# Softmax division moved from a scaled identity to GpSimd, and memory rows scaled ahead of their transposes

## The chip, the cores and the metric

One core of one Trainium2 chip runs the whole program in one launch. The metric is the device time of the program in microseconds (us). Five engines run their own instruction streams and meet at semaphores: TensorE (PE; its weight loads are listed as PEld), VectorE (DVE), ScalarE (ACT), GpSimd (POOL) and SyncE (SP, which here only starts transfers).

## The reference, cut to what matters

Two layers (`DEPTH = 2`) over 256 tokens of width 1024, everything in float32. Each layer is: a gated feed-forward block, a mixing block of three branches, a cross attention to 256 memory rows, and a second feed-forward block. The parts that the change touches are the two softmaxes of the mixing block and the normalisation of the memory rows:

```
# fox branch, 8 heads of width 64, blocks of 128 queries
logits = q k^T * 64**-0.5 + bias;  p = softmax(logits);  o = p @ v
# dsa branch, 8 heads over a shared latent c of width 128
logits = q_lat c_sel^T * 64**-0.5 + t5 bias;  p = softmax(logits);  o_lat = p @ c_sel;  o = o_lat @ w_uv
# memory cross attention
mem_h = rms_norm(mem, mem_norm[l]);  k, v = split(mem_h @ w_mkv)
```

## The kernel before, in words

Every weight is read once from HBM, 1 MB (a "unit") at a time into a ring of three slots. ScalarE copies a unit to its rounded part `w_hi` (L491), VectorE subtracts to get the rest `w_lo` (L499), and TensorE multiplies three times per tile (hi by hi, lo by hi, hi by lo; L1500, L1522, L1537 and L1575/L1577). The order of the work on each engine is written out by hand and is the same for all units.

In the mixing block a stream of 16 attention steps (`STREAM = 16`, positions `s` = 0 to 15, plus 3 to drain) is woven between weight units. A step is two heads of one block of 128 queries. Steps 0 to 7 are the fox branch, 8 to 15 the dsa branch; within each, the first four see 128 keys per head and the last four 256. At position `s` TensorE does in this order: `pt` of step s-1 (transposes the probabilities), `pv` of s-2 (times the values), `uv` of s-3 (dsa only), `qk` of s (the logits), `ql` of s+1 (dsa only), for s = 13 to 16 `mt` (normalises and transposes a quarter of the memory rows), and then one weight unit of 48 matmuls, the "filler" `FILL[s]`.

The softmax of a step: VectorE takes the logits from PSUM into `lg` and their minimum (L1336 or L1345, L1349), ScalarE takes the exponential in place with its row sum (L1013), VectorE the reciprocal `ri` (L1361). GpSimd then builds a 128 by 128 identity scaled by `ri` for each of the two heads (`over_sum`, L750), and TensorE multiplies the unscaled `lg` with it, as an ordinary float32 matmul (L1696), which divides and transposes at once. ScalarE copies the result to `pt` (L789). After L750 GpSimd adds the causal mask to a bias (L705, steps 1 to 3) or makes the next `t5_score` (L717, from step 7 on). VectorE in the same position splits a weight unit in two parts (L499), the second right behind the reciprocal, and picks the top keys (L1375, L1377) or merges branches (L1192, L1196, L1199).

The memory rows `mem_x`: ScalarE takes squares at s = 10 (L1026); GpSimd makes `rstd` and with it a scaled identity `diag` (`power`, L697); TensorE at s = 13 to 16 multiplies the rows with `diag` (`rows_over_rms`, L1455).

PSUM results of these jobs turn through 4 banks in the order of the jobs: a job may start when the job four before it has been taken out of its bank (`wait_free`, `wait_jobs`). The names to follow in the code are `over_sum`, `over_sum_ready`, `power`, `rows_over_rms` and `wait_free`. Further on, in the cross attention, the kernel has already a `pe.transpose` of probabilities that VectorE has divided in place (L1773).

Of the kernel before, what the change touches and what calls it, by code (L numbers as in the profile page):

```python
# [23 lines left out]
ACT = mybir.ActivationFunctionType  # L24
# [3 lines left out]
P = 128  # L28
# [207 lines left out]
def block_kernel(nc, t, out):  # L236

    ctx = ExitStack()
    with ctx:
# [3 lines left out]
        def at(name, shape, dtype=F32, over=None, skip=0):  # L243

            nbytes = 4 * int(np.prod(shape[1:]))
            if over is None:
                start = at.top
                at.top += (nbytes + 31) // 32 * 32
            else:
                start = place[over] + skip  # L250
            place[name] = start
            return nc.alloc_sbuf_tensor_at(name, shape, dtype, offset=start)
# [33 lines left out]
        mem_q = at("mem_q", [P, BT, SEQ], over="kc")  # L286
        junk = at("junk", [P, 2 * TT, 512], over="qc")
        qi = at("qi", [P, BT, SEQ])
        over_sum = at("over_sum", [P, 2, 2, P], over="qi")
        t5_score = at("t5_score", [P, 2, 2, SEQ], over="qc")  # L290
        vc = at("vc", [P, TT, BW])
        ki = at("ki", [P, SEQ])
# [62 lines left out]
        def sem(name):  # L355
            return ctx.enter_context(nc.semaphore(name))
# [52 lines left out]
        lg_ready = sem("lg_ready")  # L409
        exp_ready = sem("exp_ready")  # L410
        ri_ready = sem("ri_ready")
        over_sum_ready = sem("over_sum_ready")
        causal_ready = sem("causal_ready")
        score_ready = sem("score_ready")
        t5_score_ready = sem("t5_score_ready")
# [249 lines left out]
        def _(g):  # L665
# [17 lines left out]
            def power(l, n, tt, diagonal=True):  # L683

                step = (SUMS_OF + SUMS_OF[:1])[n] // TT
                g.wait_ge(ssq_ready, l * SSQ + (sum(SUMS_OF[:n]) + step * (tt + 1)))
                if step == 2:
                    g.tensor_tensor(ms[:, tt:tt + 1], ssq[:, tt, 0:1], ssq[:, tt, 1:2], ALU.add)  # L688
                else:
                    g.tensor_tensor(ms[:, tt:tt + 1], ssq[:, tt, 0:1], one_lat[:], ALU.mult)  # L690
                g.drain()
                g.tensor_scalar(ms[:, tt:tt + 1], ms[:, tt:tt + 1], EPS, None, ALU.add)
                g.drain()
                e = g.tensor_tensor(rstd[:, tt:tt + 1], ms[:, tt:tt + 1], minus_half[:], ALU.pow)
                if diagonal:
                    g.drain()  # L696
                    e = g.tensor_scalar(diag[:, tt, :], ident[:], rstd[:, tt:tt + 1], None, ALU.mult)  # L697
                    if n in (0, 5, 6):
                        e = g.tensor_scalar(half_rstd[:, tt:tt + 1], rstd[:, tt:tt + 1], 0.5, None, ALU.mult)
                e.then_inc(rstd_ready, 1)  # L700
# [40 lines left out]
            for l in range(DEPTH):  # L741
                for n in (1, 2):
                    for tt in range(TT):
                        power(l, n, tt, n != 2)
                for s in range(STREAM):
                    if s == 0:
                        g.wait_ge(bias_landed, l * 32 + 32)
                        causal_bias(0)
                    g.wait_ge(ri_ready, l * STREAM + s + 1)
                    g.tensor_tensor(over_sum[:, s % 2, :, :], ident[:].unsqueeze(1).to_broadcast([P, 2, P]),  # L750
                                    ri[:, s % 2, :].unsqueeze(2).to_broadcast([P, 2, P]), ALU.mult)\
                     .then_inc(over_sum_ready, 1)
                    if 0 < s < 4:
                        causal_bias(s)
                    if 8 <= s + 1 < STREAM:
                        bias_and_score(l, s + 1)
                    if s == 10:
                        for tt in range(TT):
                            power(l, 3, tt)
                for n in range(4, len(SUMS_OF) + 1):  # L760
                    for tt in range(TT):
                        power(l, n, tt)
# [3 lines left out]
        def _(a):  # L766
# [128 lines left out]
            for l in range(DEPTH):  # L895
# [87 lines left out]
                for s in range(STREAM + 3):  # L983
                    if 0 <= s - 1 < STREAM:
                        k = s - 1
                        n_s = (k % 8) // 4 + 1
                        copy_out(l, ("pt", k), pt[:, k % 2, :, 0:n_s, :],
                                 ps(("pt", k))[:, 0:2 * n_s * P].rearrange("p (h c t) -> p h c t", h=2, t=P))
                    if 0 <= s - 2 < STREAM:
                        k = s - 2  # L990
                        blk, h, base, m = slot_of(k)
                        if k < 8:
                            wait_done(a, l, ("pv", k))
                            a.activation(o_hi[1][base:base + HD, m:m + 2, blk * P:blk * P + P],
                                         ps(("pv", k))[base:base + HD, 0:2 * P].rearrange("p (h t) -> p h t", h=2),
                                         ACT.Copy).then_inc(o_part, 1)
                        else:
                            copy_out(l, ("pv", k), ol[:, k % 2, :, :],
                                     ps(("pv", k))[:, 0:2 * P].rearrange("p (h t) -> p h t", h=2))
                    if 8 <= s - 3 < STREAM:  # L1000
                        k = s - 3
                        blk, h, base, m = slot_of(k)
                        wait_done(a, l, ("uv", k))
                        a.activation(o_hi[0][base:base + HD, m:m + 2, blk * P:blk * P + P],
                                     ps(("uv", k))[base:base + HD, 0:2 * P].rearrange("p (h t) -> p h t", h=2),
                                     ACT.Copy).then_inc(o_part, 1)
                    if s >= 1:
                        splits(a, split_hi, l, FILL[s - 1])
                    if s < STREAM:
                        s_len = P * ((s % 8) // 4 + 1)  # L1010
                        a.wait_ge(lg_ready, l * STREAM + s + 1)
                        for j in range(2):
                            e = a.activation(lg[:, s % 2, j, 0:s_len], lg[:, s % 2, j, 0:s_len], ACT.Exp, scale=-1.0,  # L1013
                                             bias=nm[:, s % 2, j:j + 1], accum_out=sm[:, s % 2, j:j + 1])
                        e.then_inc(exp_ready, 1)
                    if 8 <= s + 1 < STREAM:
                        k = s + 1
                        copy_out(l, ("ql", k), ql[:, k % 2, :, :],
                                 ps(("ql", k))[:, 0:2 * P].rearrange("p (h t) -> p h t", h=2))
                    if s == 8:  # L1020

                        a.dma_start(mem_x[:], t["mem"][0].rearrange("(a p) d -> p a d", p=P)).then_inc(mem_landed, 16)
                    if s == 10:
                        a.wait_ge(mem_landed, l * 16 + 16)
                        for b in range(2 * TT):
                            a.activation(mem_junk[:, b, :], mem_x[:, b // 2, (b % 2) * 512:(b % 2) * 512 + 512], ACT.Square,  # L1026
                                         scale=D ** -0.5, accum_out=ssq[:, b // 2, b % 2:b % 2 + 1]).then_inc(ssq_ready, 1)
                    if 13 <= s < 17:
                        for k in (2 * (s - 13), 2 * (s - 13) + 1):
                            norm_hi(l, 4, k, mem_hi, ("mt", k // 2))  # L1030
                    filler(l, FILL[s])
# [415 lines left out]
        def _(pe):  # L1447
# [188 lines left out]
            for l in range(DEPTH):  # L1636
# [50 lines left out]
                for s in range(STREAM + 3):  # L1687
                    if 0 <= s - 1 < STREAM:
                        k = s - 1
                        n_s = (k % 8) // 4 + 1  # L1690
                        pe.wait_ge(over_sum_ready, l * STREAM + k + 1)
                        wait_free(pe, l, ("pt", k))
                        for j in range(2):
                            for c in range(n_s):
                                col = (j * n_s + c) * P
                                mm = pe.matmul(ps(("pt", k))[:, col:col + P], lg[:, k % 2, j, c * P:c * P + P],  # L1696
                                               over_sum[:, k % 2, j, :], start=True, stop=True)
                        mm.then_inc(job_done, 1)
                    if 0 <= s - 2 < STREAM:
                        k = s - 2  # L1700
# [38 lines left out]
                                           qb[base:base + HD, m + j, blk * P:blk * P + P], start=True, stop=True)  # L1739
                        mm.then_inc(job_done, 1)  # L1740
                    if 13 <= s < 17:
                        pe.wait_ge(rstd_ready, l * 12 + 8)
                        wait_free(pe, l, ("mt", s - 13))
                        for k in (2 * (s - 13), 2 * (s - 13) + 1):
                            for tt in range(TT):
                                mm = rows_over_rms(l, ("mt", s - 13), k, tt, mem_x)
                        mm.then_inc(job_done, 1)
                    filler(l, FILL[s])
                for name in AFTER:
# [61 lines left out]
```

## Time and profile before

| what | value |
|---|---|
| median of 3 runs | 1472.14 us (1470.92 to 1473.11) |
| the profiled execution's own time | 1473.94 us |
| its span in the trace | 1472.0 us |
| PE busy | 1432.3 us, 97% |
| DVE / ACT / POOL busy | 64% / 53% / 9% |
| granted TensorE clock | 0.993 of full speed |
| mean HBM rate | 165 GB/s |

The span is what the trace covers; the time has some 2 us more around it. A busy share is an average over stages, and a matmul's record overlaps the next one's: what a matmul takes of the engine is the distance from one start to the next, not the duration in the record. Times in rows of the timeline are from the span's start; a row with "x4" holds four instructions one after the other, and its second column is from the first start to the last end. Rows in which idle time precedes name it in brackets with what ended it.

### The profile page before, as it was taken

The numbers are of one execution on the slowest core, as the hardware profiler recorded it, in microseconds if no ns is written. First come the engines' busy times: TensorE is split into PE (matmuls) and PEld (weight loads), VectorE is DVE, ScalarE is ACT, GpSimd is POOL, SyncE is SP. The second block draws the span as 40 slices with busy tenths as digits, with TensorE's granted clock in tenths as the row PEclk, the third lists the DMA queues.
The fourth block names the chain that finished last, engine by engine and source line by source line (L and its number), as shares of the span: only waits on it lengthen the run. The fifth ranks groups of instructions, "written<-read, shape, count | busy, mean of one in ns | idle before, by whom it ended". The sixth has DMA issues, their size and how long they took to land.

```text
span 1472.0 us, 24395 instructions
## 1 busy us (share of the span) xinstructions
PE 1432.3 (97%) x9101; PEld 1282.8 (87%) x9101; DVE 935.2 (64%) x1451; ACT 786.3 (53%) x1394; POOL 127.0 (9%) x223
## 2 busy tenths in 40 slices
PE   6999989999999999999999999999999999999997
PEld 5888879989999898888888888898998999888886
DVE  5666665866546557666676666667755465666665
ACT  5545555655544456545565545565555445655553
POOL 2010000021310100000000000000233001000001
PEclk9999999999999999999999999999999999999999
DMA  8677654644335535666566667454353454466661
GB/s 230 186 203 215 193 146 140 200 144 144 115 115 172 172 116 171 189 182 199 172 185 187 184 187 220 142 165 152 115 166 94 132 182 144 139 185 191 183 188 72
DMA packets 286066, 243.41 MB, mean 165 GB/s; under 512 B 14280, under 2 KB 263544, under 8 KB 285984
## 3 DMA queue, kind: packets, MB, share of 16 engines
q1 hardware_dynamic: 283856, 236.77, 53.1%
q10 hardware_dynamic: 1600, 4.25, 0.9%
q0 software_dynamic: 528, 1.26, 0.5%
q8 instruction: 56, 0.92, 0.2%
q14 instruction: 26, 0.21, 0.0%
HBM read 241.18 MB, written 1.27 MB: 165 GB/s over the span
## 4 chain that ended last, share of the span: by engine, by line
issue 62%; PE 29%; DVE 4%; POOL 1%; POOLq 1%; DMA 1%; DVEq 1%; ACT 1%; ACTq 0%
PE work L1500 16%; PE work L1575 2%; PE work L1522 2%; PE work L1696 1%; PE work L1577 1%; PE acc L1537 1%; PE work L1730 1%; PE work L1706 1%; PE work L1727 1%; DVE w_lo L499 1%; POOLq L696 1%; PE acc L1455 1%; POOL diag L697 1%; DVE score L1302 1%; PE work L1644 0%
## 5 line engine op out<-in xcount | busy, mean ns | idle before, releaser
L499 DVE TENSOR_TENSOR w_lo<-raw,w_hi 128x1024 fp32r<-128x1024 f32 x444 | 532.8, 1221 | 103.4 <-ACT w_hi L491 102.2
L1575 PE MATMUL work<-act,w_hi 128*128 128x512 f32 x1408 | 499.0, 398 | 8.3 <-DVE w_lo L499 4.3
L491 ACT ACTIVATE w_hi<-raw 128x1024 fp32r<-128x1024 f32 x444 | 452.2, 1051 | 26.0 <-PE acc L1537 25.6
L1577 PE MATMUL work<-act,w_lo 128*128 128x256 f32 x1408 | 396.0, 281 | 0.0
L1575 PEld LDWEIGHTS work<-act,w_hi 128*128 128x128 f32 x1408 | 265.5, 189 | 72.1 <-issue 9.3
L1500 PE MATMUL work<-act,w_hi 128*128 128x256 f32 x1696 | 316.6, 285 | 4.2 <-DVE act L1097 3.3
L1500 PEld LDWEIGHTS work<-act,w_hi 128*128 128x128 f32 x1696 | 267.4, 191 | 11.4 <-issue 7.5
L1577 PEld LDWEIGHTS work<-act,w_lo 128*128 128x128 f32 x1408 | 267.4, 190 | 1.6
L1500 PE MATMUL work<-act,w_lo 128*128 128x256 f32 x848 | 239.8, 283 | 0.0
L796 ACT ACTIVATE gu_s<-work 128x256 f32<-128x256 f32 x176 | 58.0, 381 | 209.4 <-PE work L1577 209.4
L1500 PEld LDWEIGHTS work<-act,w_lo 128*128 128x128 f32 x848 | 162.5, 192 | 0.0
L1119 DVE TENSOR_TENSOR gu_s<-gu_s,work 128x256 f32<-128x256 f32 x176 | 66.2, 417 | 138.6 <-ACT gu_s L796 138.6
L1537 PE MATMUL acc<-w_hi,h_hi 128*128 128x512 f32 x320 | 125.4, 392 | 0.0
L1537 PE MATMUL acc<-w_lo,h_hi 128*128 128x512 f32 x320 | 125.3, 392 | 0.0
L1537 PE MATMUL acc<-w_hi,h_lo 128*128 128x512 f32 x320 | 125.2, 391 | 0.0
L806 ACT ACTIVATE h_hi<-h_f 128x256 fp32r<-128x256 f32 x80 | 33.4, 418 | 102.6 <-PE acc L1537 86.9
L688 POOL TENSOR_TENSOR ms<-ssq 128x1 f32<-128x1 f32 x22 | 4.9, 225 | 892.6 <-ACT junk L771 892.6
L1537 PEld LDWEIGHTS acc<-w_hi,h_lo 128*128 128x128 f32 x320 | 60.1, 188 | 13.3
L1537 PEld LDWEIGHTS acc<-w_hi,h_hi 128*128 128x128 f32 x320 | 60.1, 188 | 13.3
L1537 PEld LDWEIGHTS acc<-w_lo,h_hi 128*128 128x128 f32 x320 | 60.1, 188 | 11.4
L1138 DVE TENSOR_TENSOR h_lo<-h_f,h_hi 128x256 fp32r<-128x256 f32 x80 | 33.7, 421 | 49.5 <-ACT h_hi L806 49.5
L750 POOL TENSOR_TENSOR over_sum<-ident,ri 128x256 f32<-128x256 f32 x32 | 42.1, 1315 | 251.5 <-DVE ri L1361 251.5
(230 smaller groups left out, 1837.5 us busy)
## 6 DMA issues: line engine op xcount, KB each, us to landing
raw<-in_ffn_w_gu SPq DMA_DIRECT2D x176, 512.0 KB, 5.0
raw<-in_w_in SPq DMA_DIRECT2D x52, 1024.0 KB, 5.2
raw<-in_ffn_w_down SPq DMA_DIRECT2D x44, 1024.0 KB, 5.0
raw<-in_w_branch SPq DMA_DIRECT2D x12, 1024.0 KB, 5.0
raw<-in_w_mkv SPq DMA_DIRECT2D x8, 1024.0 KB, 5.3
raw<-in_w_out SPq DMA_DIRECT2D x8, 1024.0 KB, 4.8
raw<-in_w_mq SPq DMA_DIRECT2D x4, 1024.0 KB, 5.5
raw<-in_w_mo SPq DMA_DIRECT2D x4, 1024.0 KB, 4.9
```

The lines of the kernel that those rows point to most:

```text
L491: eng.activation(halves(w_hi, slot, kind, part), halves(raw, slot, kind, part), ACT.Copy)\
L499: eng.tensor_tensor(halves(w_lo, slot, kind, part), halves(raw, slot, kind, part), halves(w_hi, slot, kind, part).bitcast(F32), ALU.subtra ...
L750: g.tensor_tensor(over_sum[:, s % 2, :, :], ident[:].unsqueeze(1).to_broadcast([P, 2, P]), ri[:, s % 2, :].unsqueeze(2).to_broadcast([P, 2 ...
L796: a.activation(gu_s[:, c, g, :], work[:, 2 * c + g, SEQ:2 * SEQ], ACT.Copy).then_inc(cross_ready, 1)
L806: a.activation(dst[:, c, :], h_f[:, c, :], ACT.Copy).then_inc(h_hi_ready, 1)
L1119: v.tensor_tensor(gu_s[:, c, g, :], gu_s[:, c, g, :], work[:, 2 * c + g, 0:SEQ], ALU.add)\
L1138: v.tensor_tensor(lo[:, c, :], h_f[:, c, :], hi[:, c, :].bitcast(F32), ALU.subtract)\
L1500: mm = pe.matmul(out_ps, ww[:, slot, first:first + width], xx[:, k, :], start=(k == 0 and n == 0), stop=(k == kn - 1 and n == 2))
L1522: mm = pe.matmul(out_ps(tt), xx[:, k, tt * P:tt * P + P], ww[:, slot, k * 256 + cols[0]:k * 256 + cols[1]], start=(k == 0 and n == 0), sto ...
L1537: mm = pe.matmul(acc[:, tt, nh * 512:nh * 512 + 512], xx[:, k0 + kk, tt * P:tt * P + P], ww[:, slot, kk * D + nh * 512:kk * D + nh * 512 + ...
L1575: pe.matmul(work[:, 2 * c + g, :], w_hi[:, slot, at_w:at_w + P], act[:, :, k, :], start=(k == 0), stop=False, skip_group_check=True)
L1577: mm = pe.matmul(work[:, 2 * c + g, 0:SEQ], w_lo[:, slot, at_w:at_w + P], act_hi[:, k, :], start=False, stop=(k == KT - 1), skip_group_che ...
```

## The change

GpSimd no longer builds `over_sum`; it multiplies `lg` in place by the reciprocal, over as many keys as the step has (2 x 128 or 2 x 256 elements per partition). TensorE then transposes `lg` with the plain identity. For the memory rows, `power` leaves out the scaled identity; at s = 11 ScalarE multiplies each of the two row tiles by its `rstd` in place, and TensorE at s = 13 to 16 transposes the scaled rows with the plain identity.

```diff
-                    g.tensor_tensor(over_sum[:, s % 2, :, :], ident[:].unsqueeze(1).to_broadcast([P, 2, P]),
-                                    ri[:, s % 2, :].unsqueeze(2).to_broadcast([P, 2, P]), ALU.mult)\
-                     .then_inc(over_sum_ready, 1)
+                    s_len = P * ((s % 8) // 4 + 1)
+                    g.tensor_tensor(lg[:, s % 2, :, 0:s_len], lg[:, s % 2, :, 0:s_len],
+                                    ri[:, s % 2, :].unsqueeze(2).to_broadcast([P, 2, s_len]), ALU.mult)\
+                     .then_inc(p_ready, 1)
...
-                            power(l, 3, tt)
+                            power(l, 3, tt, False)
...
+                    if s == 11:
+                        a.wait_ge(rstd_ready, l * 12 + 8)
+                        for tt in range(TT):
+                            a.activation(mem_x[:, tt, :], mem_x[:, tt, :], ACT.Copy, scale=rstd[:, tt:tt + 1])\
+                             .then_inc(mem_scaled, 1)
...
-                        pe.wait_ge(over_sum_ready, l * STREAM + k + 1)
+                        pe.wait_ge(p_ready, l * STREAM + k + 1)
                         wait_free(pe, l, ("pt", k))
...
-                                mm = pe.matmul(ps(("pt", k))[:, col:col + P], lg[:, k % 2, j, c * P:c * P + P],
-                                               over_sum[:, k % 2, j, :], start=True, stop=True)
+                                mm = pe.transpose(ps(("pt", k))[:, col:col + P], lg[:, k % 2, j, c * P:c * P + P], ident[:])
...
-                        pe.wait_ge(rstd_ready, l * 12 + 8)
+                        pe.wait_ge(mem_scaled, (l + 1) * TT)
                         wait_free(pe, l, ("mt", s - 13))
...
-                                mm = rows_over_rms(l, ("mt", s - 13), k, tt, mem_x)
+                                mm = pe.transpose(ps2(("mt", s - 13))[:, k % 2, tt * P:tt * P + P],
+                                                  mem_x[:, tt, k * P:(k + 1) * P], ident[:])
```

## Rows read from the trace of the kernel before

**Rows 1.** The page's first part: busy us, share of the span, instructions.
```profile
PE 1432.3 (97%) x9101; PEld 1282.8 (87%) x9101; DVE 935.2 (64%) x1451; ACT 786.3 (53%) x1394; POOL 127.0 (9%) x223
```

**Rows 2.** Windows: attention of layer 0; span, busy PE, PEld, DVE, ACT, POOL, PEclk, DMA, GB/s.
```profile
289.00:447.00 158.00, 155.86 (x1218) 145.83 (x1217) 95.55 (x176) 83.75 (x179) 37.02 (x35) 1.00 0.40 129
```

**Rows 3.** Source views of L1696, L1455 and L1773: count, duration ns min/median/max.
```profile
L1696 PE MATMUL work<-over_sum,lg x192: 270/275/377, 297.0 to 1153.7; 128*128 128x128 f32 x192
L1455 PE MATMUL work<-diag,mem_x x64: 273/275/377, 401.0 to 1156.3; 128*128 128x128 f32 x64
L1773 PE MATMUL work<-ident,lg x32: 270/272/273, 529.7 to 1260.5; 128*128 128x128 f32 x32
```

**Rows 4.** Timeline of PE: groups of L1696 and of transposes, each with what follows.
```profile
312.10 0.60 PE L1696 MATMUL work<-over_sum,lg 128*128 128x128 f32 x4
312.63 0.65 PE L1706 MATMUL work<-pt,vc 128*64 128x128 f32 x4
...
397.33 1.05 PE L1696 MATMUL work<-over_sum,lg 128*128 128x128 f32 x8
398.22 0.61 PE L1710 MATMUL work<-pt,c_nat 128*128 128x128 f32 x4
...
529.74 1.03 PE L1773 MATMUL work<-ident,lg 128*128 128x128 f32 x8
530.53 0.36 PE L1522 MATMUL work<-w_hi,mem_hi 128*128 128x256 f32 x1
```

**Rows 5.** Timeline of PE at s = 2: `pv` of step 0.
```profile
305.03 0.65 PE L1706 MATMUL work<-pt,vc 128*64 128x128 f32 x4 [0.24 <-ACT vc L789]
```

**Rows 6.** Timeline of PE at s = 14, and PE's row of the waits.
```profile
412.35 1.16 PE L1455 MATMUL work<-diag,mem_x 128*128 128x128 f32 x8
413.81 0.39 PE L1500 MATMUL work<-act,w_hi 128*128 128x256 f32 x1 [0.29 <-DVE o_lo L1355]
...
PE work L1500 <- DVE o_lo L1355: 0.9, 4, 0.3
```

**Rows 7.** Timeline of POOL at s = 2 and 3 (L750).
```profile
309.15 1.84 POOL L750 TENSOR_TENSOR over_sum<-ident,ri 128x256 f32<-128x256 f32 x1 [5.78 <-DVE ri L1361]
...
316.78 0.61 POOL L750 TENSOR_TENSOR over_sum<-ident,ri 128x256 f32<-128x256 f32 x1 [5.09 <-DVE ri L1361]
```

**Rows 8.** Timeline at s = 6: L750, the split beside it, and `pt` behind.
```profile
342.25 1.84 POOL L750 TENSOR_TENSOR over_sum<-ident,ri 128x256 f32<-128x256 f32 x1 [8.30 <-DVE ri L1361]
342.41 1.21 DVE L499 TENSOR_TENSOR w_lo<-raw,w_hi 128x1024 fp32r<-128x1024 f32 x1
...
345.04 1.05 PE L1696 MATMUL work<-over_sum,lg 128*128 128x128 f32 x8
```

**Rows 9.** Timeline at s = 12 (layer 0): POOL, DVE, and `qk` of step 13.
```profile
394.21 1.21 DVE L499 TENSOR_TENSOR w_lo<-raw,w_hi 128x1024 fp32r<-128x1024 f32 x1
...
395.85 1.28 POOL L717 TENSOR_TENSOR t_score<-t,score 128x512 f32<-128x512 f32 x1
396.21 1.47 DVE L1199 TENSOR_TENSOR merged<-merged,gate 128x512 f32<-128x512 f32 x1
...
397.61 0.68 DVE L1196 SCALAR_TENSOR_TENSOR gate<-gate,work 128x512 f32<-128x512 f32 x1
...
398.36 0.69 DVE L1199 TENSOR_TENSOR merged<-merged,gate 128x512 f32<-128x512 f32 x1
...
399.34 1.13 PE L1730 MATMUL work<-c_t,ql 128*128 128x256 f32 x4
```

**Rows 10.** Timeline of ACT at s = 11 and 12, and `w_hi`'s row of the groups.
```profile
384.22 0.36 ACT L789 ACTIVATE ql<-work 128x256 f32<-128x256 f32 x1
...
388.56 0.60 ACT L870 ACTIVATE gate<-work 128x512 f32<-128x512 f32 x1 [3.98 <-PE work L1500]
...
L491 ACT ACTIVATE w_hi<-raw 128x1024 fp32r<-128x1024 f32 x440 | 448.8, 1053 | 26.0 <-PE acc L1537 25.6
```

**Rows 11.** Timeline of POOL: the last `power` of the memory rows.
```profile
381.78 0.62 POOL L697 TENSOR_SCALAR diag<-ident,rstd 128x128 f32<-128x128 f32 x1 [0.17 <-issue]
```

More of the change, by code:

```diff
@@ L288, in block_kernel @@
         qi = at("qi", [P, BT, SEQ])
-        over_sum = at("over_sum", [P, 2, 2, P], over="qi")
         t5_score = at("t5_score", [P, 2, 2, SEQ], over="qc")
@@ L411, in block_kernel @@
         ri_ready = sem("ri_ready")
-        over_sum_ready = sem("over_sum_ready")
+        p_ready = sem("p_ready")
+        mem_scaled = sem("mem_scaled")
         causal_ready = sem("causal_ready")
```

## The prediction

> **What bounds the kernel now.** I read the page's busy shares first: TensorE works 97% of the span, no other engine above 64% [rows 1]. Then the window of the stretch that holds the attention steps of layer 0 (layer 1 repeats it), since a mean over the whole span may hide a stage with another limit: there TensorE is busy 155.9 of 158.0 us, VectorE 96 and ScalarE 84 [rows 2]. So TensorE sets the pace in the changed stretch too, and what the change takes from TensorE's stream shortens the kernel unless an engine that hands it work becomes late. The weights arrive at 129 GB/s there [rows 2], under the 165 of the whole span, so loads have room. Third, the source views and the timeline of the changed instructions give their price, and the brackets on PE's rows show where it waits.
>
> **TensorE, the terms.** The program issues 96 division matmuls (per layer 8 steps of 2 and 8 steps of 4), but the trace has 192 records for L1696; 32 for the memory rows, but 64 records for L1455. The `pe.transpose` of L1773, with the same kind of operand (`lg` against the plain identity), is issued 32 times and has 32 records [rows 3]. So one float32 matmul runs as two passes and a transpose as one. The mean duration, 275 and 272 ns, tells nothing of the difference; distances do. Eight passes of L1696 last 1.05 us up to the last end, so (1.05 - 0.275)/7 = 0.111 us from start to start; eight transposes last 1.03, so (1.03 - 0.272)/7 = 0.108 us; and the next group starts 0.89 us after the first of eight passes, 0.79 after the first of eight transposes [rows 4]. One pass of 0.11 us is saved for each matmul: 0.22 us in a step of two (four passes, now 0.53 us to the next group), 0.44 us in a step of four. If all of it reached the end: 128 x 0.11 = 14.1 us.
>
> The Trainium skill, "TensorE: Matmul & The Clock Gate", Part 4 (PE-mode transpose), gives about 275 ns for a transpose in a kernel and says that access latency dominates it. The records here agree in length (272 ns), but the starts are 108 ns apart, so that latency overlaps in a row of transposes. By the page's figure as a price the change would lose; that is one of the rivals below.
>
> **What of it is lost in waits on PSUM banks.** A shorter group helps only if the next job may start.
> - `pt` of step 1: `pv` of step 0 waited 0.24 us for ScalarE's copy of `vc`, which starts when the filler ahead of `pt` ends [rows 5]. `pt` shortens, the wait grows by as much: 0 of 0.22.
> - `mt` at s = 13 and 14: the filler behind it needs the bank that VectorE empties at L1355, behind the logits of `qk`. At s = 14 it waited 0.29 us, and the waits' row has four such waits, 0.9 us in all: s = 13 and 14 of both layers [rows 6]. That moment hangs on `qk`, which is ahead of `mt`, so `mt`'s 0.44 us turns into waiting: 0. At s = 15 and 16 there is no such wait, 2 x 0.44.
> - `pt` of step 12: `qk` of step 13 needs the bank of the second half of `bc0`, which VectorE empties at L1199. That ends at 398.36 + 0.69 = 399.05, and `qk` starts at 399.34 [rows 9]. With 0.44 us less in front of it `qk` reaches its place at 398.90 and waits. It is lost here, and possibly more (below).
> - The other steps have no bracket and reach a bank that is free for longer.
>
> Per layer: narrow steps 0, 2, 3, 8, 9, 10, 11, 7 x 0.22 = 1.54; wide steps 4 to 7, 13, 14, 15, 7 x 0.44 = 3.08; `mt` 0.88; together 5.5. Two layers: 11.0 us.
>
> **GpSimd, the division.** For narrow steps it multiplies 256 elements as before (1.52 us or so). For wide steps it is 512 instead of 256, which no row of L750 shows. From below, nothing: it might cost the same. The nearest row is L717 on 512 elements, 1.28 us [rows 9]; from above, twice the longest L750, 3.68 us [rows 7]. The records of L750 are of two kinds, 0.61 and 1.84 us for one shape [rows 7]. At s = 6 it begins at 342.25, VectorE's split L499 runs from 342.41 to 343.62, and L750 ends at 344.09, that is 0.47 us after L499 [rows 8]; at s = 12 the pattern is turned round, L1199 starts at 396.21 beside a running L717 and lasts 1.47 instead of 0.69 us, to 0.55 us after the end of L717 at 397.13 [rows 9]. So the two engines exclude each other in these operations, and the net length is some 0.6 us for 256 and 1.28 us for 512. I take 1.28, since it is a two-input operation of this size on this engine with a broadcast operand.
>
> The Trainium skill, "SBUF — State Buffer", section "SBUF: two separate sides", calls the pair of ports that VectorE and GpSimd share an exclusive lock, held for the whole instruction by whoever starts first. The rows agree, and the rule speaks against this change: the wide division holds VectorE off for longer.
>
> Its deadline is `pt`. At s = 6 the split ends at 343.62, so the division ends at 344.90, and `pt` starts at 345.04 [rows 8]: 0.14 us to spare. At s = 12 it ends at 395.42 + 1.28 = 396.70 against 397.33 [rows 4, 9]. Steps 4 and 15 resemble these; in the other wide steps GpSimd comes first or `pt` is later. So nothing on the path, narrowly; if the cover were gone each further 0.1 us costs 0.1 us a step.
>
> Behind the division are queued, on GpSimd, `t5_score` of the next step (L717), needed only at the next `qk`, and on VectorE, by the exclusion, the second split and what follows. That is free except at s = 12: L1199 now starts when the division ends (396.70) or, if L717 takes its turn first, at 397.98. In the first order it ends at 397.4, L1196 of the second half at 398.3, and the second L1199 waits for L717 (397.4 to 398.7) and ends at 399.4: `qk` of step 13 is 0.06 us later than before. In the second the ends are 398.7, 399.4 and 400.1: 0.75 us later. I take 0.3 us for each layer, 0.6 in all; the bounds are 0.1 and 1.5.
>
> **ScalarE, the memory rows.** Two copies with a scale over 128x1024 elements; the nearest row has 1.053 us for that size, so 2.1 us a layer. They stand behind the copy of `ql` at 384.22 + 0.36 = 384.58, and the next instruction, the gate at 388.56, sat idle 3.98 us in wait of TensorE [rows 10]. 384.58 + 2.1 = 386.7: hidden, with 1.9 us over. The new wait for `rstd` ends at once: GpSimd had ended even the `diag` that now goes at 382.40 [rows 11]. `mt` needs the rows at s = 13, about 401. Without cover it would be 4.2 us for both layers on ScalarE, and it is the bound of this term; I take 0. `diag` off GpSimd (0.62 us each) gives nothing: TensorE used it 20 us later. No DMA is added or moved.
>
> **Sum.** -11.0 + 0.6 = -10.4 us. The profiled execution took 1473.94 us (span 1472.0 plus 1.9 around), so 1463.5; the median of the runs shown is 1.8 us lower, 1472.14, which gives **1461.7 us**. Changes under 0.2% (2.9 us) count as none.
>
> **The rivals.**
> 1. *The division is twice as long*, 2.56 us net. For it: the rows of GpSimd are rough, and in-place operands are not L717's. Against: 0.47 us of L750 behind the split. Room behind the end of the split: 345.04 - 343.62 = 1.42 us at s = 6 and 397.33 - 395.42 = 1.91 at s = 12 [rows 4, 8, 9]; two wide steps of each kind wait: 2 x 1.14 + 2 x 0.65 = 3.6 us a layer, 7.2 in all. -11.0 + 7.2 = -3.8: **1468.3**. Chance 0.09.
> 2. *The division ends above the time before.* The same place with twice the longest record, 3.68 us: 2 x 2.26 + 2 x 1.77 = 8.1 a layer, 16.1 in all, +5.1: **1477.2**. It decides from 4T - 6.66 = 5.5, T = 3.04 us. Against: L717's 1.28. Chance 0.02.
> 3. *Transposes do not overlap* and cost their 272 ns each: a group of four 1.09 instead of 0.89, of two 0.54 instead of 0.53, 16 + 8 groups of four: 24 x 0.2 = +4.8 us: **1477**. Against: the eight of L1773 in 1.03 us. Chance 0.02.
> 4. *Nothing changes on TensorE*, the transpose being run as two passes: **1472 to 1473**. Against: 32 records for 32. Chance 0.03.
> 5. *Waits I count as lost are not*: VectorE's chain moves forward too, and all 14.1 us arrive: **1458.0**. Against: the brackets. Chance 0.08.
>
> **Chances and range.** Forecast 0.76, own range 1459.5 to 1464.5 (the bounds at s = 12 and 1 us for the medians). Faster: 0.76 + 0.09 + 0.08 = 0.93; same 0.03; slower 0.04. For 8 in 10 I widen to rival 5 and towards rival 1: 1458.5 to 1466.5.
>
> **What the profile after would show.** L1696 and the `mt` transposes with 96 and 32 records, eight passes now four, `pt` to `pv` about 0.31 us narrow and 0.45 to 0.54 wide; PE busy some 13 us less. The wide division 1.3 us where GpSimd comes first and 2.0 to 2.5 where the split does, no PE wait on it beyond the first step's. The wait on `o_lo` L1355 grows from 0.9 us to about 2.5; `qk` of step 13 gets a wait. ScalarE's copies end before 388. The prediction is wrong if `pt` waits for the division in many steps, or if transposes are more than 0.15 us apart.

## The result, and the profile after

| | before | after |
|---|---|---|
| median, first comparison (6 runs each) | 1471.53 us | 1463.06 us |
| median, second comparison (18 and 5 runs) | 1471.47 us | 1461.31 us |
| ratio after/before, 95% interval | | 0.9943 [0.9931, 0.9956]; again 0.9921 [0.9907, 0.9934] |
| profiled execution: time, span | 1473.94, 1472.0 us | 1461.06, 1459.3 us |
| PE busy | 1432.3 us | 1415.9 us |

By the ratios the change gains 8.4 us in the first comparison (interval 6.5 to 10.2) and 11.6 in the second (9.7 to 13.7); the medians themselves are 8.5 and 10.2 us apart. 10.4 was forecast (1461.7 us).

The comparison that holds from run to run is a stretch of the trace: from the first `qk` of a layer to the first matmul of `mk0`, 16 steps and 18 fillers further. It is 157.98 us in layer 0 of before (288.94 to 446.92 in its timeline) and 152.12 after. The timeline of PE of the changed kernel, the two ends:

```profile
287.94 0.71 PE L1732 MATMUL work<-kc,qc 64*128 64x128 f32 x4
...
440.06 0.39 PE L1506 MATMUL work<-mem_hi,w_hi 128*128 128x256 f32 x1
```

That is 5.86 us. In layer 1 it was 159.69 us before and is 152.10 after. Of the 1.71 us by which layer 1 of before is longer than its layer 0, 1.50 are one filler in which the granted clock fell (last section) and 0.2 stand in front of `qk` of step 13 (told at s = 12, below). So layer 0 is taken as the measure: 5.86 us a layer, 11.7 in all. The stage behind it, to the transposes of the second feed-forward block (552.01 us in before), is 105.09 us in both profiles; the stages outside the stretch differ by up to 1 us either way (layer 0's first feed-forward 190.48 and 189.84, layer 1's second 187.31 and 188.23), as they do between two profiles of one kernel. So, within that scatter, the trace has the gain in the changed stretch alone.

The source views of the transposes after, against [rows 3] (L1702 was L1696, L1751 stands for L1455's matmuls of `mem_x`):

```profile
L1702 PE MATMUL work<-ident,lg x96: 270/272/328, 296.1 to 1140.6; 128*128 128x128 f32 x96
...
L1751 PE MATMUL work<-ident,mem_x x32: 272/273/330, 396.5 to 1142.6; 128*128 128x128 f32 x32
```

128 records have gone, and the durations are as before: it is the count that fell, not the length. The weight loads fell by the same 128 (PEld x9101 to x8973), so what goes is a pass together with its load; no run separates the two. The timeline of PE, a narrow `pt` group and a wide one, against [rows 4]:

```profile
310.85 0.38 PE L1702 MATMUL work<-ident,lg 128*128 128x128 f32 x2
311.16 0.65 PE L1711 MATMUL work<-pt,vc 128*64 128x128 f32 x4
...
393.01 0.60 PE L1702 MATMUL work<-ident,lg 128*128 128x128 f32 x4
393.45 0.61 PE L1715 MATMUL work<-pt,c_nat 128*128 128x128 f32 x4
```

0.31 us to the next group in place of 0.53, 0.44 in place of 0.89. What did not arrive stands in PE's waits after. Of the third row [rows 6] had 0.9 us; the first row belongs to other stages:

```profile
PE work L1506 <- DVE act L1103: 4.0, 4, 1.3
PE work L1702 <- POOL lg L751: 2.9, 2, 1.5
PE work L1506 <- DVE o_lo L1361: 2.9, 4, 0.8
PE work L1711 <- ACT vc L790: 0.9, 2, 0.5
...
PE work L1735 <- DVE merged L1205: 0.3, 2, 0.2
```

The wait on GpSimd, 2.9 us in 2 times, is that of the first step of each layer, as before. No other step waits for the division.

Laid over each other from the first `qk`, the fillers of layer 0 start earlier by these amounts (us, worked out from the starts in the two timelines; step 1 is the `pt` in position 2, and so on):

| part | forecast | measured |
|---|---|---|
| `pt` of step 0 | 0.22 | 0.26 |
| `pt` of step 1 (waits for `vc`) | 0 | 0.00 |
| `pt` of steps 2, 3 | 0.44 | 0.45 |
| `pt` of steps 4 to 7 | 1.76 | 1.69 |
| `pt` of steps 8 to 11 | 0.88 | 0.92 |
| `pt` of step 12 and `mt` at s = 13 | 0, less 0.3 | 0.24 |
| `pt` of step 13 and `mt` at s = 14 | 0.44 | 0.44 |
| `pt` of steps 14, 15, `mt` at s = 15, 16 | 1.76 | 1.85 |
| sum | 5.2 | 5.86 (rounded parts 5.85) |

### The profile page after: what moved, and what is told of

Read it like the earlier page. It is cut to its first block, busy times and chain, and to the rows that moved or that the text cites. A ratio compares the mean times of both kernels' runs of the same rounds, so it can differ in the third digit from the quotient of the medians.

```text
span 1459.3 us, 24135 instructions
## 1 busy us (share of the span) xinstructions
PE 1415.9 (97%) x8973; PEld 1265.0 (87%) x8973; DVE 935.3 (64%) x1451; ACT 789.1 (54%) x1398; POOL 131.6 (9%) x219
## 4 chain that ended last, share of the span: by engine, by line
issue 62%; PE 29%; DVE 4%; POOL 1%; POOLq 1%; DMA 1%; ACT 1%; DVEq 1%; ACTq 0%
PE work L1506 17%; PE work L1581 2%; PE work L1528 2%; PE work L1583 1%; PE acc L1543 1%; PE work L1735 1%; PE work L1711 1%; PE work L1732 1%; POOLq L696 1%; PE work L1702 1%; DVE w_lo L499 1%; POOL diag L697 1%; DVE score L1308 1%; PE acc L1461 1%; PE work L1650 0%
## 5 line engine op out<-in xcount | busy, mean ns | idle before, releaser
L751 POOL TENSOR_TENSOR lg<-lg,ri 128x256 f32<-128x256 f32 (+1 forms) x32 | 48.9, 1528 | 239.6 <-DVE ri L1367 239.6
L1543 PEld LDWEIGHTS acc<-w_lo,h_hi 128*128 128x128 f32 x320 | 60.1, 188 | 11.7
```

The lines of the kernel that those rows point to most:

```text
L751: g.tensor_tensor(lg[:, s % 2, :, 0:s_len], lg[:, s % 2, :, 0:s_len], ri[:, s % 2, :].unsqueeze(2).to_broadcast([P, 2, s_len]), ALU.mult)\
L1543: mm = pe.matmul(acc[:, tt, nh * 512:nh * 512 + 512], xx[:, k0 + kk, tt * P:tt * P + P], ww[:, slot, kk * D + nh * 512:kk * D + nh * 512 + ...
```

## The experiments

All stretches are from the first `qk` to `mk0`. Where the text speaks of the clock's fall, the granted clock had fallen in one filler of that layer, which makes the stretch 1.5 us longer; that is told in the last section, and the other layer is compared. Each ratio is to runs of before taken beside that kernel, so kernels of different experiments are compared by their stretches or ratios, not by their medians.

**1. The changed kernel again.**

> The changed kernel once more, in more rounds. In the two profiles the attention stretch (first qk to the first matmul of mk0) went from 157.98 and 159.69 us to 152.12 and 152.10, 1.7 us of it in layer 1 being a filler that was slow once in the profile of before. Theory (one TensorE pass of 0.11 us less per matmul, less the waits): 2 x 5.86 = 11.7 us less in the medians too, ratio 0.992. Rival (something of it is given back in other stages, as the medians of 1471.53 and 1463.06 would have it): 8.4 us less again, ratio 0.9943, and another stage longer by 3 us in its profile.

Measured: 1461.31 us, ratio 0.9921 [0.9907, 0.9934], which is 11.6 us less (the medians are 10.2 apart); stretches 152.12 and 153.62 us, the stages behind them 105.09 again. This interval holds the 11.7 us of the trace and not the rival's 8.4. Nothing is given back elsewhere in the profile: layer 1's 153.62 is the fall of the clock. Why the first six runs had 8.4, with an interval that doesn't hold 11.7, isn't shown: their mean granted clocks were 0.991 to 0.993, those of these five 0.992 to 0.996.

**2. The probabilities alone.** As after, but

```diff
-                            power(l, 3, tt, False)
+                            power(l, 3, tt)
...
-                                mm = pe.transpose(ps2(("mt", s - 13))[:, k % 2, tt * P:tt * P + P],
-                                                  mem_x[:, tt, k * P:(k + 1) * P], ident[:])
+                                mm = rows_over_rms(l, ("mt", s - 13), k, tt, mem_x)
```

and without ScalarE's copies.

> Only the probabilities: division on GpSimd and transposes in L1702; the memory rows as before, with diag. Theory (passes saved less waits): the memory part is worth 2 x 0.44 us a layer at s = 15 and 16 only, so this kernel keeps 5.0 of 5.9 us a layer: 10.0 us under before, the stretch 153.0 us. Rival (the memory transposes save all their passes, 1.76 us a layer): 8.2 us under before, the stretch 153.9 us.

Measured: 1462.05 us, ratio 0.9933 [0.992, 0.9947]; stretches 153.09 and 153.10 us, wait on `o_lo` 0.9 us. 4.89 us a layer from the probabilities, where the theory had 5.0.

**3. The memory rows alone.** As before, with the edits of `power`, ScalarE's copies and the `mt` transposes.

> Only the memory rows: scaled by ScalarE, transposed with the identity; over_sum as before. Theory: at s = 13 and 14 the filler waits for o_lo L1355 in place of the passes saved, at s = 15 and 16 two times 0.44 us arrive: 1.8 us under before, wait on o_lo 2.7 us in place of 0.9. Rival: all 16 passes a layer arrive, 3.5 us under before. Rival 2: the copies of 2.2 us on ScalarE are in the way: no gain or slower.

Measured: 1469.15 us, ratio 0.9984 [0.9974, 0.9995]; stretches 156.85 and 157.03 us, wait on `o_lo` 2.9 us. 1.13 and 0.95 us arrive. The `mt` groups themselves bring 0.44 us at s = 15, 0.50 at s = 16 and nothing at s = 13 and 14, that is 0.94 of the 1.76 us of passes in a layer; the rest is lost in the wait. What the stretches show beside it is not of this edit: the filler at s = 15 is 0.2 us shorter in both layers, and layer 1 loses 0.2 us in front of `qk` of step 13, as it does in before.

**4. Both edits, but ordinary matmuls with the identity.**

```diff
-                                mm = pe.transpose(ps(("pt", k))[:, col:col + P], lg[:, k % 2, j, c * P:c * P + P], ident[:])
+                                mm = pe.matmul(ps(("pt", k))[:, col:col + P], lg[:, k % 2, j, c * P:c * P + P], ident[:],
+                                               start=True, stop=True)
```

> The changed kernel with ordinary float32 matmuls against the identity in place of both transposes (two passes again); GpSimd still divides, ScalarE still scales. Theory: the whole gain is TensorE's passes, so this takes the time of before within 1 us (stretch 158.0 us) with the waits on o_lo back at 0.9 us. Rival: the division in place of over_sum costs or gains by itself: over 2 us away from before, with waits of TensorE on the division.

Measured: 1471.48 us, ratio 0.9993 [0.9982, 1.0004]; stretches 158.01 and 158.00 us, and the wait on `o_lo` is back at 0.9 us. The source view of L1702 has 192 records again:

```profile
L1702 PE MATMUL work<-ident,lg x192: 270/275/377, 295.6 to 1149.6; 128*128 128x128 f32 x192
```

The move of the division and of the scaling costs and gains nothing by itself; the whole gain is the pass that TensorE leaves out in its transpose mode.

**5. Every transpose of the probabilities twice.**

```diff
-                                mm = pe.transpose(ps(("pt", k))[:, col:col + P], lg[:, k % 2, j, c * P:c * P + P], ident[:])
+                                mm = [pe.transpose(ps(("pt", k))[:, col:col + P], lg[:, k % 2, j, c * P:c * P + P], ident[:]) for _ in range(2)][-1]
```

> The changed kernel with every transpose of the probabilities issued twice into the same place (96 more). Theory (a transpose in a row costs its 0.108 us, start to start): 48 x 0.108 = 5.2 us more a layer, of which the waits on vc (0.47) and on merged (0.17) take back 0.4: stretch 152.1 + 4.8 = 156.9 us, time 9.6 us over the changed kernel. Rival (a transpose costs its 0.272 us): 13 us a layer, 26 in all.

Measured: 1468.47 us, ratio 0.9973 [0.9963, 0.9984]; stretches 156.77 and 156.80 us, 4.7 more a layer. 48 transposes cost 4.7 us net of the waits that they fill, some 0.1 us each: the start-to-start distance is the price, the 272 ns of the record are not. By the ratios this kernel is 7.6 us over the changed one, where 9.6 was expected and the stretches have 9.3; with 0.001 of uncertainty in each ratio (1.5 to 2 us) that doesn't contradict them.

**6. One more multiplication ahead of the wide divisions.**

```diff
+                    if s_len == 2 * P:
+                        g.tensor_tensor(lg[:, s % 2, :, 0:s_len], lg[:, s % 2, :, 0:s_len],
+                                        ones[:, 0:2].unsqueeze(2).to_broadcast([P, 2, s_len]), ALU.mult)
+                        g.drain()
```

> The changed kernel with one more GpSimd multiplication (by ones) ahead of the division in the wide steps, that is 1.04 us more there with the drain. Theory (the division is hidden with the room of the trace, 0.5 us at s = 6, 0.6 at s = 4, 1.0 at s = 12, 0.9 at s = 15, over 1.7 elsewhere): TensorE waits 0.6 + 0.5 + 0.1 + 0.2 us a layer, and VectorE's merging at s = 12 is held up so that qk of step 13 waits up to 1 us more: 3 to 6 us over the changed kernel. Rival 1 (it was never near the path): within 1 us. Rival 2 (all eight wide steps pay in full): 16 x 1.04 = 17 us.

Measured: 1465.74 us, ratio 0.9958 [0.9946, 0.9971]; in layer 1, where the clock held, 155.36 us, 3.24 more than after. Layer 0 has 156.51 with the clock's fall of 1.48, so 2.9 more; the layers differ before `pt` of step 12, where TensorE waited 0.37 and 0.72 us for the division. TensorE's wait on POOL is 6.5 us in 10 times in place of 2.9 in 2. Step 6 in its timeline:

```profile
1059.81 2.27 POOL L752 TENSOR_TENSOR lg<-lg,ones 128x512 f32<-128x512 f32 x1 [5.70 <-DVE ri L1371]
...
1062.22 1.04 POOL L755 TENSOR_TENSOR lg<-lg,ri 128x512 f32<-128x512 f32 x1
...
1063.31 0.66 PE L1706 MATMUL work<-ident,lg 128*128 128x128 f32 x4 [0.56 <-POOL lg L755]
```

The division is hidden with about the room that the trace shows; four of the eight wide steps of a layer run out of it.

**7. VectorE empties `uv`'s bank ahead of the logits.** In VectorE's loop the block with L1361 (`o_lo` of step s-3) moves in front of the block that waits for `qk` of s; nothing else changes.

> The changed kernel with VectorE's L1361 (it empties the bank of uv) ahead of the logits of the position in place of behind them; VectorE idles there for TensorE's qk. Theory (the memory passes at s = 13 and 14 were lost in TensorE's wait on that bank): the waits of 0.66 and 0.80 us go, 1.4 us a layer, stretch 150.7 us, 2.8 us under the changed kernel. Rival: TensorE then waits for something else there (mt's or ol's bank), gain under 1 us.

Measured: 1455.25 us, ratio 0.9885 [0.9866, 0.9904]; stretches 150.15 and 150.12 us; once more, in five runs:

> The kernel olo_first once more, for an interval of its own: stretch 150.15 us (151.6 in a layer in which the granted clock falls behind the first division), 2 x 1.97 = 3.9 us under the changed kernel, ratio 0.9895 to before. Rival: the ratio of 0.9885 of four runs was luck and it is at 0.991 or above.

Measured: 1455.73 us, ratio 0.9897 [0.9881, 0.9914]; stretches 151.64 (with the clock's fall) and 150.16. The timeline at s = 13, of the changed kernel and then of this one:

```profile
396.48 0.66 PE L1751 MATMUL work<-ident,mem_x 128*128 128x128 f32 x4
...
397.80 0.39 PE L1506 MATMUL work<-act,w_hi 128*128 128x256 f32 x1 [0.66 <-DVE o_lo L1361]
```

```profile
393.13 0.42 DVE L1337 TENSOR_TENSOR o_lo<-work,o_hi 64x256 fp32r<-64x256 f32 x1 [0.41 <-ACT o_hi L1005]
...
394.00 0.69 DVE L1358 SCALAR_TENSOR_TENSOR lg<-work,t_score 128x512 f32<-128x512 f32 x1 [0.45 <-PE work L1735]
...
394.53 0.65 PE L1751 MATMUL work<-ident,mem_x 128*128 128x128 f32 x4
...
394.94 0.36 PE L1506 MATMUL work<-act,w_hi 128*128 128x256 f32 x1
```

L1337 runs in time that VectorE spent waiting for `qk`. From `mt` to the filler it was 1.32 us and is 0.41: 0.91 gained where the bracket said 0.66; at s = 14 it is 1.06 where the bracket said 0.80. A bracket counts from the modelled end of the last matmul. The group's record ends 0.66 us after its start, but without the wait the filler starts 0.41 us after it, so the bracket leaves out 0.25 us, and a loss of this kind is read from starts. That makes 1.97 us a layer, more than the 1.4 expected.

**8. In addition, `t5_score` ahead of the division.**

```diff
+                    if 8 <= s + 1 < STREAM:
+                        g.wait_ge(lg_ready, l * STREAM + s + 1)
+                        bias_and_score(l, s + 1)
                     g.wait_ge(ri_ready, l * STREAM + s + 1)
...
-                    if 8 <= s + 1 < STREAM:
-                        bias_and_score(l, s + 1)
```

> As the kernel before in this call, and GpSimd makes the next t5_score ahead of the division, once the logits of the position are out, in place of behind it. Theory: at s = 12 VectorE's L1205 is no longer held up by L717, TensorE's wait of 0.17 us before qk of step 13 goes, 0.2 to 0.3 us a layer: stretch 150.4 us, 0.5 us under the kernel before it. Rival: L717 now stands beside the first split of VectorE and in front of the division, so the division is late: a TensorE wait on it in some steps and no gain.

Measured: 1456.49 us, ratio 0.9892 [0.9873, 0.9912]; layer 1's stretch 150.14 us, layer 0's 151.62 with the clock's fall. Nothing gained, and the wait before `qk` of step 13 stays at 0.17: my theory of it fell. The rival fell too, for TensorE's wait on the division is still that of the first steps, 2.9 us in 2 times.

**9. The bank handed back one instruction earlier.** On top of 7, L1202, the only reader of the PSUM bank, frees it in place of L1205, and a new semaphore says when `gate` is free, the buffer in which ScalarE hands VectorE its factor for the merge. (`ba`, `bc` and `bb` are the three branches, `ba0` and `bc0` the first of their weight units.) The first version also had a drain, in which VectorE waits for its own writes, behind each half of `ba`.

> The kernel with L1361 ahead of the logits, and in the merging VectorE hands the PSUM bank back after the one instruction that reads it (L1202) in place of the next (L1205); a semaphore of its own says when the gate buffer is free. The kernel olo_first had TensorE waiting 0.18 us before qk of step 13, the end of VectorE's L1202 and L1205, which ran without a hold by GpSimd. Theory (that wait is VectorE's own chain of 2 x 0.7 us behind TensorE's last matmul of bc0, and the bank is what it hands on): the wait goes, and with it 0.2 to 0.3 us a layer, stretch 149.9 us in place of 150.15. Rival (the wait was for something else that comes at the same time): stretch unchanged.

Measured: 1456.22 us, ratio 0.9904 [0.9889, 0.9919]; stretches 150.24 and 150.22. The wait went and `qk` of step 13 gained 0.24 us, but `ql` of step 8 came 0.3 us later, behind the drain. Without it (ScalarE's waits for the new semaphore are left out here):

```diff
                         v.scalar_tensor_tensor(out=g2, in0=g2, scalar=1.0, in1=ps2((name, half)), op0=ALU.add,
-                                               op1=ALU.mult)
+                                               op1=ALU.mult).then_inc(bank_of((name, half)), 1)
                         v.drain()
-                        e = v.tensor_tensor(m2, m2, g2, ALU.add)
-                        e.then_inc(bank_of((name, half)), 1)
+                        v.tensor_tensor(m2, m2, g2, ALU.add).then_inc(gate_used, 1)
```

> As release_early, but without the drain that it put between the two halves of ba0 and ba1 (the gate's semaphore now counts the halves of bc and bb alone). In release_early the wait before qk of step 13 went and gave 0.24 us, and the drain held the second L1197 back by 0.21 us, so that ql of step 8 came 0.28 us later. Theory: without the drain the 0.24 us stays, stretch 149.9 us in both layers where the clock does not fall. Rival: 150.15 us as in olo_first.

Measured: 1454.94 us, ratio 0.9883 [0.9866, 0.9899]; stretches 149.91 and 149.92 us, as expected. The timeline in front of `qk` of step 13, layer 1: `qk` (L1737) now starts before L1208, which was L1205, has ended:

```profile
1107.15 0.69 DVE L1208 TENSOR_TENSOR merged<-merged,gate 128x512 f32<-128x512 f32 x1
...
1107.72 1.13 PE L1737 MATMUL work<-c_t,ql 128*128 128x256 f32 x4
```

This is the best version: 8.1 us a layer under before in the stretch, 16 us in the medians. From 7 its medians can't be told apart; the stretches can.

**10. ScalarE's copies doubled.** Each scaled copy preceded by a copy by 1 and a drain.

> The changed kernel with each of ScalarE's scaled copies of the memory rows preceded by a copy of the same rows by 1, 4.4 us in place of 2.2 us a layer at s = 11. Theory (the copies lie in ScalarE's idle time before the gate, 1.89 us of it left): the gate starts 0.3 to 0.5 us late, TensorE has room for that, stretch 152.1 us as before. Rival (ScalarE's copies are on the path): stretch 154.3 us.

Measured: one run, 1466.5 us; stretches 153.61 and 153.56, both with the clock's fall. That fall is over before the filler of s = 2: laid over the changed kernel from there to the end, every filler has the same distance within 0.05 us. ScalarE goes from its last copy to `gate` without idle time, and TensorE doesn't notice. The term is nothing even with twice the work.

## Why the prediction was right, point by point

**One pass for two.** Right, and shown by 4 and 5: the passes are the whole gain, 0.22 us in narrow and 0.44 to 0.45 in wide steps. PE's busy time fell by 16.4 us where some 13 was forecast.

**Lost in waits on banks.** `pt` of step 1 and `mt` at s = 13 and 14 gave 0, as forecast, and experiment 7 gave the latter back. One such wait I had missed: `ql` of step 8 needs `ba0`'s bank and lost 0.11 us of step 6's 0.44. (It was in experiment 9 that `ql` moved with VectorE's work on `ba0`.)

**The division.** The mechanism was right, the size too large: 1.04 us net, not 1.28. Timeline at s = 5 and 6, against [rows 8]:

```profile
331.19 1.04 POOL L751 TENSOR_TENSOR lg<-lg,ri 128x512 f32<-128x512 f32 x1 [5.75 <-DVE ri L1367]
331.60 1.71 DVE L499 TENSOR_TENSOR w_lo<-raw,w_hi 128x1024 fp32r<-128x1024 f32 x1
...
339.65 2.27 POOL L751 TENSOR_TENSOR lg<-lg,ri 128x512 f32<-128x512 f32 x1 [7.42 <-DVE ri L1367]
339.81 1.21 DVE L499 TENSOR_TENSOR w_lo<-raw,w_hi 128x1024 fp32r<-128x1024 f32 x1
...
342.43 0.60 PE L1702 MATMUL work<-ident,lg 128*128 128x128 f32 x4
```

Whoever is first holds the other off: at s = 5 the split takes 1.71 us in place of 1.21, at s = 6 the division 2.27 in place of 1.04. It ends 0.51 us before `pt`, where 0.14 was forecast.

**The failed term: s = 12.** The sum had "I take 0.3 us for each layer" lost beyond `pt`'s 0.44. Measured: 0.24 gained. The first error needed no experiment. By [rows 9] VectorE ended at 399.05, and the rows after show that `qk` starts 0.15 us behind that end (394.66, 394.81), so before it could have started at 399.20 in place of 399.34: of the 0.44 us, 0.14 were free even with VectorE as it was. The rest is that VectorE's second half begins 0.20 in place of 0.28 us after `pt`. The timeline of the changed kernel, against [rows 9]:

```profile
391.90 0.69 DVE L1205 TENSOR_TENSOR merged<-merged,gate 128x512 f32<-128x512 f32 x1
391.97 1.77 POOL L717 TENSOR_TENSOR t_score<-t,score 128x512 f32<-128x512 f32 x1
...
393.21 0.69 DVE L1202 SCALAR_TENSOR_TENSOR gate<-gate,work 128x512 f32<-128x512 f32 x1 [0.62 <-PE work L1506]
...
393.97 0.69 DVE L1205 TENSOR_TENSOR merged<-merged,gate 128x512 f32<-128x512 f32 x1
...
394.81 1.10 PE L1735 MATMUL work<-c_t,ql 128*128 128x256 f32 x4 [0.17 <-DVE merged L1205]
```

The shorter division ends as L1205 begins, VectorE goes first, and it is L717 that is held (1.77 us in place of 1.28). VectorE then even waits 0.62 us for TensorE; the second half runs without a hold, in 2 x 0.7 us plus gaps, and that chain sets `qk`. I had put a wait down to contention between two engines that was the plain length of the second one's work; 8 and 9 tell them apart. This term is 0.54 of the 0.66 us between 5.2 and 5.86; the rest is small differences.

Contention at this place was real, though: in the profile of before, layer 1 pays for it. The timeline there:

```profile
1119.34 1.28 POOL L717 TENSOR_TENSOR t_score<-t,score 128x512 f32<-128x512 f32 x1
1119.70 1.47 DVE L1199 TENSOR_TENSOR merged<-merged,gate 128x512 f32<-128x512 f32 x1
...
1121.10 0.67 DVE L1196 SCALAR_TENSOR_TENSOR gate<-gate,work 128x512 f32<-128x512 f32 x1
...
1122.68 1.10 PE L1730 MATMUL work<-c_t,ql 128*128 128x256 f32 x4
```

VectorE comes to this place some 0.36 us later than in layer 0 (it has 0.44 us of idle time at L1349 that nothing in the profile explains), and L717 holds L1199 to 1121.17. So the second L1196 begins 0.64 us after `pt` (1120.46) in place of 0.28, and `qk` starts 0.2 us later. Without the 0.78 us of the hold L1199 would have been done before `pt`. The changed kernel has the same idle time in its layer 1 and doesn't pay for it: there VectorE's wait for TensorE, 0.62 us in layer 0, shrinks to 0.27, and `qk` keeps its distance.

**ScalarE.** 2.18 us in place of 2.1, and 1.89 of the 3.98 us of idle time left:

```profile
380.40 2.18 ACT L1032 ACTIVATE mem_x<-mem_x,rstd 128x1024 f32<-128x1024 f32 x2
...
384.48 0.60 ACT L871 ACTIVATE gate<-work 128x512 f32<-128x512 f32 x1 [1.89 <-PE work L1506]
```

**The rivals.** None came. Experiment 6 is near rival 1 (2.08 us net in place of 1.04): 3.24 us a layer, where 3.6 was worked out for 2.56. Rival 5 had all 14.1 us arrive; 11.7 did.

## What to carry to other kernels

A float32 matmul against a diagonal costs TensorE two passes, a transpose with the plain identity one; where TensorE is the bound, let another engine do the scaling in its idle time. Before counting the gain, follow each shortened group to the next job's wait, from start to start: here 1.8 us of passes turned into waiting on a bank, and emptying it earlier in VectorE's idle time brought 3.9 us, those and 2.1 us of waiting that the kernel before had too, at no cost that a later filler shows. And when a wait is put down to contention, check first whether the waiting chain is not simply that long: here, after the change, it was; in one layer of before the hold cost 0.2 us.

## What the runs showed of the hardware that I had not expected

Runs of one kernel spread by up to 6 us (1469.19 to 1475.32 in 18 runs of before), and a part of that has a place. In some layers of some profiles the filler right behind the first step's division, where TensorE had idled 1.45 us, is 1.47 to 1.50 us longer. Windows of before, layer 1 (columns as in [rows 2]), and then the same place of the changed kernel:

```profile
1019.00:1022.00 3.00, 3.00 (x19) 2.76 (x18) 2.11 (x6) 2.58 (x6) 0.00 (x0) 0.75 0.30 107
1022.00:1025.00 3.00, 3.00 (x20) 3.00 (x19) 2.78 (x9) 0.47 (x3) 2.21 (x2) 0.68 0.05 10
```

```profile
1013.00:1015.00 2.00, 2.00 (x16) 1.88 (x16) 1.39 (x4) 1.94 (x3) 0.00 (x0) 1.00 0.43 148
1015.00:1018.00 3.00, 3.00 (x27) 3.00 (x26) 2.93 (x7) 1.11 (x5) 1.58 (x2) 1.00 0.00 0
```

The granted clock is 0.75 and 0.68 as the mean of two windows of 3 us; the matmuls inside follow each other every 0.21 in place of 0.12 us for some 3.4 us, the lower of the two levels (1.2 GHz), though TensorE was never idle in them. The same 1.45 us of idle time stands before it in both, so that alone doesn't decide; what does stays open.
